# Probabilities times values in products of 512 queries: high parts in one run, low parts in another, and a head's written order anew on three engines

## The chip, the core and the metric

The kernel runs on one core of a Trainium2 chip. It is one launch of a two-layer encoder, and the metric is the device time of that launch in microseconds (us). Three runs of the kernel before gave 2706.74, 2706.79 and 2706.95 us, median 2706.79.

The engines named in the rows are PE (TensorE matmul), PEld (its weight loads), DVE (VectorE), ACT (ScalarE), POOL (GpSimd) and SP (which issues the DMAs). Each works through its own list of instructions in the order in which the kernel wrote them, and waits at semaphores for the others.

## The reference

Each of two layers does a mix (attention beside a short convolution), a squared-ReLU MLP and a gated embedding, each between two RMS norms. The change touches only the last lines of the attention:

```
def one_block(args):                       # 128 queries, all 1024 keys, 8 heads
    qn_b, qr_b = args
    sc = (einsum('bqhd,bkhd->bhqk', qn_b, k_nope) + einsum('bqhr,bkr->bhqk', qr_b, k_rope))
    w = softmax(sc * scale, axis=-1)
    return einsum('bhqk,bkhd->bqhd', w, v)
...
attn = latent_attention(q_nope, q_rope, k_nope, k_rope, v)
mix = concatenate([group_rms_norm(attn, ...), group_rms_norm(conv, ...)]) 
x = x + rms_norm(mix @ w_out[i], g_post_mix[i])
```

There are 1024 tokens, 8 heads of 64 value channels, 2 layers. All is float32.

## The kernel before, in words

**Splitting.** Every float32 operand of a matmul is kept as a high part, rounded by ACT (`copy`, line 1665), and a low part, the rest, which DVE computes from the two (line 2156, and line 2402 for the probabilities). A product of two such operands is three matmuls (lines 1146 to 1148).

**A head.** The 1024 queries of a head are 8 steps of 128. For step s, written `x.s` below:
- `score.s` (PE): 6 matmuls of 512 keys into two PSUM banks; banks 0 and 1 for even steps, 2 and 3 for odd ones.
- `least.s` (DVE, line 2395): the minimum of the negated scores over 1024 keys. Then `exp.s` (ACT, line 1877) writes the probabilities `pr` and their sum.
- `turn.s.0`, `turn.s.1` (PE, line 1355): four 128 by 128 transposes each, into bank 4 and bank 5.
- `high.s.b` (ACT, `pth`) and `low.s.b` (DVE, `ptl`, line 2402): the high and the low part of the transposed probabilities, 512 elements a partition each.
- `pv` (PE, lines 1379 and 1380): probabilities times values. The stationary operand is a 128 by 128 piece of `vv`, the moving one `pth` or `ptl`. `vv` holds zeros, the values' high part and their low part side by side, so that one matmul gives high times high in one half of the partitions and low times high in the other.

Before, `pv` takes 256 queries (G, two steps) at a time: 8 chunks of keys, each one matmul with `pth` and one with `ptl`, 128x256. `pv.h.G.part` is half of that, 8 matmuls. `pth` and `ptl` have room for two G, so steps 4 and 5 may be written while the product of steps 2 and 3 is still to come.

After `pv`, for each half t of the queries: `out` (ACT) and `sum` (DVE, line 2416) add the two halves of the partitions, `square` and `sq_high` (ACT) and `sq_low` (DVE) prepare the group norm, `var` (PE, lines 1185 and 1186) sums it, `ln` and `r` (ACT, lines 1924 and 1928) give the factor, `scale` (DVE, line 2427) applies it, and `y` (ACT, then DVE) splits the result. `den` (DVE) turns the sums of the probabilities, which SP sends out and back.

**The order.** Three tables, ATT_PE, ATT_ACT and ATT_DVE (from line 222), say in which order each engine does a head's steps. The first number is the head, relative to the current one: `pv.-1.3.0` belongs to the head before, `score.1.0` to the next. Beside the head's own work they hold the next head's keys and values (`kv`, `k`, `v`, `v_turned`) and queries (`q`, `q_low`), the split of a later head's weights (`unit.0`), and for the last head only the first output products (`mix`) and the split of their weights (`last.7.1` to `last.7.3`; `last.6.0` is in the head before it). Steps of a head that doesn't exist are left out: the first head has no `-1` work, the last no `1` work (`head_steps`, line 353).

**Waits that matter.** `turn.s` waits for `exp.s` and for `low.(s-1)` of its bank. `score.s` waits for `exp.(s-2)`. `mix.0.0` waits for `exp.6` of the last head. `var` waits for `sq_low`. `y` of t = 0 waits until SP's store of the former `y` has landed.

Of the kernel before, what the change touches and what calls it, by code (L numbers as in the profile page):

```python
# [29 lines left out]
HEADS, NOPE, ROPE, V_DIM = 8, 64, 32, 64  # L30
# [186 lines left out]
def steps(text):  # L217

    return [(word.split(".")[0],) + tuple(int(n) for n in word.split(".")[1:]) for word in text.split()]


ATT_PE = steps("""
turn.0.0.0 turn.0.0.1 score.0.2 kv.1.0 score.0.3 turn.0.1.0 turn.0.1.1 pv.-1.3.0 kv.1.1 pv.-1.3.1 turn.0.2.0
turn.0.2.1 score.0.4 pv.0.0.0 turn.0.3.0 turn.0.3.1 score.0.5 pv.0.0.1 var.-1.1 v.1 turn.0.4.0 score.0.6 q.1.0
turn.0.4.1 score.0.7 pv.0.1.0 pv.0.1.1 turn.0.5.0 turn.0.5.1 mix.0.0 q.1.1 turn.0.6.0 turn.0.6.1 mix.0.1
score.1.0 pv.0.2.0 turn.0.7.0 turn.0.7.1 mix.1.0 var.0.0 pv.0.2.1 score.1.1
""")

ATT_ACT = steps("""
high.0.0.0 high.0.0.1 exp.0.1 y.-1.0 v.1.0 k.1.0 last.7.1 exp.0.2 high.0.1.0 high.0.1.1 exp.0.3 v.1.1 k.1.1  # L230
out.-1.1 high.0.2.0 high.0.2.1 square.-1.1 sq_high.-1.1 unit.0 last.6.0 high.0.3.0 high.0.3.1 exp.0.4 ln.-1.1
last.7.2 exp.0.5 v_turned.1 high.0.4.0 high.0.4.1 r.-1.1 q.1.0 exp.0.6 y.-1.1 high.0.5.0 high.0.5.1 exp.0.7
out.0.0 high.0.6.0 high.0.6.1 square.0.0 last.7.3 sq_high.0.0 q.1.1 high.0.7.0 high.0.7.1 exp.1.0 ln.0.0 r.0.0
""")

ATT_DVE = steps("""
scale.-1.0 low.0.0.0 low.0.0.1 least.0.2 k.1.0 last.7.1 least.0.3 low.0.1.0 low.0.1.1 y.-1.0 k.1.1 sum.-1.1
low.0.2.0 low.0.2.1 sq_low.-1.1 least.0.4 low.0.3.0 low.0.3.1 den.0.0 least.0.5 unit.0 last.6.0 last.7.2
v_turned.1 least.0.6 q.1.0 low.0.4.0 low.0.4.1 scale.-1.1 least.0.7 q_low.1.0 low.0.5.0 low.0.5.1 q.1.1
sum.0.0 low.0.6.0 low.0.6.1 den.0.1 last.7.3 sq_low.0.0 least.1.0 q_low.1.1 low.0.7.0 low.0.7.1 y.-1.1  # L240
least.1.1
""")


# [108 lines left out]
def head_steps(h, order):  # L353

    for kind, ahead, *more in order:
        if kind == "last":
            if h == ahead:
                yield (kind, h, *more)
        elif kind == "mix":
            if h == HEADS - 1:  # L360
                yield (kind, h, ahead, *more)
        elif 0 <= h + ahead < HEADS:
            if not (kind in ("score", "exp", "least") and h + ahead == h + 1 == HEADS):
                yield (kind, h + ahead, *more)
# [108 lines left out]
def encoder(nc, x_in, w_units, w_head, p_in, gains, table, consts, out):  # L473
# [5 lines left out]
    def sb(name, shape, dt, where=ctx):  # L479
        return where.enter_context(nc.sbuf_tensor(name, shape, dt))  # L480

    def sem(name):
        return ctx.enter_context(nc.semaphore(name))
# [7 lines left out]
    with ctx:  # L491

        den = sb("den", [P, 2, STEPS], f32)
# [39 lines left out]
        with ExitStack() as att:  # L533
# [19 lines left out]
            vv = sb("vv", [P, 2, 8, 3 * V_DIM], f32r, att)  # L553
            pth = sb("pth", [P, 2, 8, 256], f32r, att)
            ptl = sb("ptl", [P, 2, 8, 256], f32r, att)
# [23 lines left out]
        ps = ctx.enter_context(nc.psum_tensor("ps", [P, 8, HALF], f32))  # L579
# [96 lines left out]
        t_out = sem("t_out")  # L676
        t_hi = sem("t_hi")
        t_lo = sem("t_lo")
        pv_out = sem("pv_out")
        o_sq = sem("o_sq")  # L680
        o_copy = sem("o_copy")
# [230 lines left out]
        def step(L, h, s):  # L912

            return (L * HEADS + h) * STEPS + s
# [228 lines left out]
        def _(pe):  # L1143
# [82 lines left out]
            for L in range(DEPTH):  # L1226
# [37 lines left out]
                for n in range(0 if L else SLOTS, len(IN_OUTS) + 1):  # L1264
                    if n < len(IN_OUTS):
                        w, t = IN_OUTS[n]
# [89 lines left out]
                                                   pr[:, s % 2, (4 * b + c) * P:(4 * b + c + 1) * P], ident)  # L1356
                    last.then_inc(t_out, 1)

                def values(h, a, G, part):

                    H = L * HEADS + h
                    if part == 0:
                        pe.wait_ge(t_lo, 2 * step(L, h, 2 * G + 2))
                    if (h, G, part) == (0, 0, 0):
                        pe.wait_ge(v_zero, L + 1)
                    if (G, part) == (0, 0):
                        if h + 1 < HEADS:
                            pe.wait_ge(k_lo, H * 2 + 4)
                            pe.wait_ge(v_f, H * 2 + 4)
                        else:  # L1370
                            pe.wait_ge(o_ln, H * 2 - 1)
                    if (G, part) == (2, 0):
                        if h + 1 < HEADS:
                            pe.wait_ge(q_f, H * 2 + 4)
                        else:
                            pe.wait_ge(o_ln, H * 2)
                    dst = ps[:, 6 + G // 2, (G % 2) * 256:(G % 2 + 1) * 256]
                    for c in range(4 * part, 4 * part + 4):
                        nc.tensor.matmul(dst, vv[:, a, c, V_DIM:3 * V_DIM], pth[:, G % 2, c, :], start=c == 0, stop=False)  # L1379
                        last = nc.tensor.matmul(dst, vv[:, a, c, 0:2 * V_DIM], ptl[:, G % 2, c, :], start=False, stop=c == 7)  # L1380
                    if part == 1:
                        last.then_inc(pv_out, 1)

                def variances(h, a, t):

                    O = (L * HEADS + h) * 2 + t
                    pe.wait_ge(o_sq_lo, O + 1)
                    two_passes(ps[:, 6 + t, :], ones_r[:, 2 + a, :], *square_parts(h)).then_inc(o_var, 1)
# [20 lines left out]
                def attend(h):  # L1409

                    for kind, o, *n in head_steps(h, ATT_PE):
                        a, H = o % 2, L * HEADS + h
                        if kind == "turn":
                            transposes(o, *n)
                        elif kind == "score":
                            scores(o, a, *n)
                        elif kind == "kv":
                            if n[0] == 0:
                                if h:
                                    pe.wait_ge(o_ln, H * 2 - 1)  # L1420
                                else:
                                    pe.wait_ge(q_f, H * 2 + 2)
                            else:
                                pe.wait_ge(k_lo, H * 2 + 3)
                                pe.wait_ge(v_f, H * 2 + 3)
                            keys_and_values(o, a, n[0], 6)
                        elif kind == "v":
                            pe.wait_ge(t_lo, 2 * step(L, h, 3) + 2)
                            values_by_token(o, a, 0, 5)
                        elif kind == "q":  # L1430
                            if n[0]:
                                pe.wait_ge(q_f, H * 2 + 3)
                            elif h:
                                pe.wait_ge(o_ln, H * 2)
                            queries(o, a, n[0], 7)
                        elif kind == "pv":
                            values(o, a, *n)
                        elif kind == "mix":
                            mix_first(*n)
                        elif kind == "var" and (o, n[0]) != (HEADS - 1, 1):  # L1440
                            variances(o, a, n[0])
# [216 lines left out]
        def _(act):  # L1658
# [115 lines left out]
            for L in range(DEPTH):  # L1774
# [4 lines left out]
                for n in range(8 if L else 0, len(IN_OUTS)):  # L1779
                    w, t = IN_OUTS[n]  # L1780
                    kind, j = kind_of(w)
# [99 lines left out]
                def high_of_transposed(h, s, b):  # L1881
                    G = s // 2
                    act.wait_ge(t_out, 2 * step(L, h, s) + b + 1)
                    if (h, s, b) == (0, 0, 0):
                        act.wait_ge(tap, L * 12 + 12)
                    if (h, s, b) == (0, 2, 0):
                        act.wait_ge(mix_stored, L * MIX_STORED + 128)
                    if s % 2 == 0 and b == 0 and (G >= 2 or h):
                        act.wait_ge(pv_out, (L * HEADS + h) * 4 + G - 1)
                    copy(pth[:, G % 2, 4 * b:4 * b + 4, (s % 2) * P:(s % 2 + 1) * P],  # L1890
                         ps[:, 4 + b, :].rearrange("p (c q) -> p c q", c=4)).then_inc(t_hi, 1)

# [258 lines left out]
        def _(dve):  # L2151
# [98 lines left out]
            for L in range(DEPTH):  # L2250
# [39 lines left out]
                for n in range(8 if L else 0, len(IN_OUTS)):  # L2290
                    w, t = IN_OUTS[n]
                    kind, j = kind_of(w)
# [105 lines left out]
                def low_of_transposed(h, s, b):  # L2398
                    G = s // 2
                    dve.wait_ge(t_hi, 2 * step(L, h, s) + b + 1)  # L2400
                    at = (slice(None), G % 2, slice(4 * b, 4 * b + 4), slice((s % 2) * P, (s % 2 + 1) * P))
                    V.tensor_tensor(ptl[at], ps[:, 4 + b, :].rearrange("p (c q) -> p c q", c=4),  # L2402
                                    pth[at].bitcast(f32), ALU.subtract).then_inc(t_lo, 1)
# [403 lines left out]
```

## Time and profile before

| | |
|---|---|
| median of 3 runs | 2706.79 us |
| the profiled execution | 2706.97 us, its span 2704.9 us |
| PE busy | 2691.4 us, 99% of the span |
| PEld, DVE, ACT busy | 2244.1, 1935.7, 1403.2 us |
| lines 1379 and 1380 (`pv`), PE | 512 matmuls each, 128.1 and 127.2 us busy |
| one 128x256 matmul of `pv`, one 128x512 elsewhere | 285 ns and 390 ns |
| TensorE clock granted | 9 of 10 or more in all 40 slices |

Matmuls are pipelined: the next one starts before the last one's modelled end. What a matmul costs is therefore the distance from its start to the next start, and a short wait of PE may hide between a start and a modelled end. The two attention stretches run from 220.7 to about 495 us and from 1560 to about 1833 us of the span.

### The profile page before, as it was taken

To read this page: it belongs to the slowest core of one execution; us is meant where nothing else is said; L and a number is where in the kernel's file an instruction comes from. 1 tells how busy PE (TensorE), PEld (TensorE's weight loads), DVE (VectorE), ACT (ScalarE), POOL (GpSimd) and SP (SyncE) were. 2 spreads that over 40 slices of the span, in tenths; PEclk is the share of its full clock that TensorE was granted. 3 is DMA by queue.
4 is the path that set the end of the run, shared out by engine and by line. 5 is a ranking of instruction groups with operands and counts; after the bars stand their busy time and mean duration, and the time that the engine had idled before them with its cause. 6 is when DMAs were issued, how large, how long until landed. Compare 5 with 4: busy or idle time off the path is not lost.

```text
span 2704.9 us, 34531 instructions
## 1 busy us (share of the span) xinstructions
PE 2691.4 (99%) x12854; PEld 2244.1 (83%) x12854; DVE 1935.7 (72%) x2677; ACT 1403.2 (52%) x2412; POOL 302.7 (11%) x329
## 2 busy tenths in 40 slices
PE   9999999999999999999999999999999999999999
PEld 7888888888888888888888888888888888888886
DVE  5468888476676666688866788893856676667886
ACT  5338888564333333356644488884633333333464
POOL 0230000001111101120003200000011111112000
PEclk9999999999999999999999999999999999999999
DMA  4211112532111111133232111133311111111422
GB/s 167 78 68 41 34 35 74 184 110 71 63 47 55 39 53 57 63 117 117 86 118 75 60 41 34 29 140 124 140 47 48 63 47 55 39 53 57 148 94 78
DMA packets 85941, 206.17 MB, mean 76 GB/s; under 512 B 8976, under 2 KB 37776, under 8 KB 84752
## 3 DMA queue, kind: packets, MB, share of 16 engines
q1 hardware_dynamic: 85776, 203.97, 22.3%
q8 instruction: 103, 1.69, 0.3%
q14 instruction: 62, 0.51, 0.1%
HBM read 172.42 MB, written 31.52 MB: 75 GB/s over the span
## 4 chain that ended last, share of the span: by engine, by line
PE 94%; DVE 4%; ACT 1%; issue 0%; DMA 0%; POOL 0%; SPq 0%; ACTq 0%; DVEq 0%; POOLq 0%
PE ps L1146 28%; PE ps L1148 28%; PE ps L1147 28%; PE ps L1355 4%; PE ps L1380 2%; PE ps L1379 2%; DVE wl L2156 1%; DVE nm L2395 1%; PE ps L1185 1%; PE ps L1186 1%; DVE ptl L2402 1%; PE ps L1320 0%; ACT hh L1665 0%; DVE xf L2210 0%; PE ps L1172 0%
## 5 line engine op out<-in xcount | busy, mean ns | idle before, releaser
L1146 PE MATMUL ps<-hh,wh 128*128 128x512 f32 x2160 | 845.1, 391 | 2.3 <-DVE hl L2192 1.9
L1148 PE MATMUL ps<-hh,wl 128*128 128x512 f32 x2160 | 841.4, 390 | 0.0
L1147 PE MATMUL ps<-hl,wh 128*128 128x512 f32 x2160 | 841.3, 389 | 0.0
L1665 ACT ACTIVATE wh<-raw 128x256 fp32r<-128x256 f32 (+2 forms) x510 | 318.7, 632 | 481.3 <-PE ps L1148 276.8
L2156 DVE TENSOR_TENSOR wl<-raw,wh 128x256 fp32r<-128x256 f32 (+2 forms) x510 | 366.0, 733 | 160.7 <-ACT wh L1665 160.3
L1146 PEld LDWEIGHTS ps<-hh,wh 128*128 128x128 f32 x2160 | 405.8, 188 | 87.9 <-DVE wl L2156 2.9
L1147 PEld LDWEIGHTS ps<-hl,wh 128*128 128x128 f32 x2160 | 405.8, 188 | 84.6 <-issue 1.4
L1148 PEld LDWEIGHTS ps<-hh,wl 128*128 128x128 f32 x2160 | 405.7, 188 | 84.2
L2580 DVE TENSOR_TENSOR xf<-xf,ps 128x1024 f32<-128x1024 f32 x196 | 238.5, 1218 | 122.9 <-PE ps L1148 122.7
L1146 PE MATMUL ps<-hx,wh 128*128 128x512 f32 x448 | 174.7, 390 | 0.1
L1147 PE MATMUL ps<-hx,wh 128*128 128x512 f32 x448 | 174.4, 389 | 0.0
L1148 PE MATMUL ps<-hx,wl 128*128 128x512 f32 x448 | 174.4, 389 | 0.0
L2402 DVE TENSOR_TENSOR ptl<-ps,pth 128x512 fp32r<-128x512 f32 x256 | 163.8, 680 | 8.6 <-ACT pth L1665 7.9
L1665 ACT ACTIVATE pth<-ps 128x512 fp32r<-128x512 f32 x256 | 140.2, 594 | 48.0 <-PE ps L1355 46.1
L2395 DVE TENSOR_REDUCE nm<-ps 128x1 f32<-128x1024 f32 x128 | 155.4, 1214 | 1.5 <-PE ps L1148 1.1
L1877 ACT ACTIVATE pr<-ps,nm 128x1024 f32<-128x1024 f32 x128 | 142.7, 1115 | 14.5 <-DVE nm L2395 12.6
L1355 PE MATMUL ps<-cst,pr 128*128 128x128 f32 x1024 | 137.6, 274 | 1.1 <-DVE ptl L2402 0.9
L1379 PE MATMUL ps<-pth,vv 128*128 128x256 f32 x512 | 128.1, 285 | 0.0
L1355 PEld LDWEIGHTS ps<-cst,pr 128*128 128x128 f32 x1024 | 116.5, 140 | 14.0 <-issue 2.9
L1380 PE MATMUL ps<-ptl,vv 128*128 128x256 f32 x512 | 127.2, 283 | 0.0
L2699 POOL TENSOR_TENSOR spare<-raw 128x256 f32<-128x256 f32 x56 | 44.0, 785 | 722.7 <-DMA raw<-w_units 722.7
L1702 ACT ACTIVATE sq<-xf 128x512 f32<-128x512 f32 x168 | 102.8, 622 | 39.4 <-DVE accy L2186 12.3
(240 smaller groups left out, 4304.4 us busy)
## 6 DMA issues: line engine op xcount, KB each, us to landing
raw<-w_units SPq DMA_DIRECT2D x170, 512.0 KB, 3.4
raw<-w_units SPq DMA_DIRECT2D x112, 256.0 KB, 3.0
x_mid<-xf SPq DMA_DIRECT2D x4, 2048.0 KB, 7.9
xf<-x_mid SPq DMA_DIRECT2D x4, 2048.0 KB, 8.1
hh<-mix_hi SPq DMA_DIRECT2D x14, 512.0 KB, 6.1
hl<-mix_lo SPq DMA_DIRECT2D x14, 512.0 KB, 6.8
stage<-w_head SPq DMA_DIRECT2D x16, 320.0 KB, 3.3
mix_hi<-cyh SPq DMA_DIRECT2D x8, 512.0 KB, 2.6
```

The source lines that it names most:

```text
L1146: nc.tensor.matmul(dst, ah, bh, start=start, stop=False, skip_group_check=joins)
L1147: nc.tensor.matmul(dst, ah, bl, start=False, stop=False, skip_group_check=joins)
L1148: return nc.tensor.matmul(dst, al, bh, start=False, stop=stop, skip_group_check=joins)
L1355: last = nc.tensor.transpose(ps[:, 4 + b, c * P:(c + 1) * P], pr[:, s % 2, (4 * b + c) * P:(4 * b + c + 1) * P], ident)
L1379: nc.tensor.matmul(dst, vv[:, a, c, V_DIM:3 * V_DIM], pth[:, G % 2, c, :], start=c == 0, stop=False)
L1380: last = nc.tensor.matmul(dst, vv[:, a, c, 0:2 * V_DIM], ptl[:, G % 2, c, :], start=False, stop=c == 7)
L1665: return nc.scalar.activation(dst, src, ACT.Copy, **more)
L1877: nc.scalar.activation(pr[:, s % 2, :], ps[:, 2 * (s % 2):2 * (s % 2) + 2, :].rearrange("p b n -> p (b n)"), ACT.Exp, bias=nm[:, s % 2:s % ...
L2156: return V.tensor_tensor(dst, whole, high.bitcast(f32), ALU.subtract)
L2395: V.tensor_reduce(nm[:, s % 2:s % 2 + 1], ps[:, 2 * (s % 2):2 * (s % 2) + 2, :].rearrange("p b n -> p (b n)"), AX.X, ALU.min).then_inc(s_l ...
L2402: V.tensor_tensor(ptl[at], ps[:, 4 + b, :].rearrange("p (c q) -> p c q", c=4), pth[at].bitcast(f32), ALU.subtract).then_inc(t_lo, 1)
L2580: V.tensor_tensor(f, f, ps[:, bank:bank + 2, :], ALU.add).then_inc(down_add, 1)
```

## The change

`pv` becomes two steps, `pv_high.h.t.part` and `pv_low.h.t.part`, each for 512 queries (t) and half of the chunks: four matmuls of 128x512. `pv_high` needs only the high parts, `pv_low` the low ones. Since one product now reads both places of `pth` or `ptl`, the two places are no longer used in turns: ACT may write the next steps' high parts after `pv_high` of the same chunks, DVE the low parts after `pv_low` (each by halves of the chunks). The three tables are written anew.

```
 ATT_PE = steps("""
-turn.0.0.0 turn.0.0.1 score.0.2 kv.1.0 score.0.3 turn.0.1.0 turn.0.1.1 pv.-1.3.0 kv.1.1 pv.-1.3.1 turn.0.2.0
...
+turn.0.0.0 turn.0.0.1 pv_low.-1.1.0 pv_low.-1.1.1 score.0.2 turn.0.1.0 turn.0.1.1 kv.1.0 score.0.3 turn.0.2.0
...
-                def values(h, a, G, part):
+                def values(h, a, t, part, high):
 
                     H = L * HEADS + h
-                    if part == 0:
-                        pe.wait_ge(t_lo, 2 * step(L, h, 2 * G + 2))
-                    if (h, G, part) == (0, 0, 0):
+                    pe.wait_ge(t_hi if high else t_lo, 2 * step(L, h, 4 * t + 3) + part + 1)
+                    if (h, t, part) == (0, 0, 0):
                         pe.wait_ge(v_zero, L + 1)
-                    if (G, part) == (0, 0):
+                    if (t, part, high) == (0, 0, True):
                         if h + 1 < HEADS:
                             pe.wait_ge(k_lo, H * 2 + 4)
                             pe.wait_ge(v_f, H * 2 + 4)
...
-                    dst = ps[:, 6 + G // 2, (G % 2) * 256:(G % 2 + 1) * 256]
+                    dst = ps[:, 6 + t, :].rearrange("p (g n) -> p g n", g=2)
                     for c in range(4 * part, 4 * part + 4):
-                        nc.tensor.matmul(dst, vv[:, a, c, V_DIM:3 * V_DIM], pth[:, G % 2, c, :], start=c == 0, stop=False)
-                        last = nc.tensor.matmul(dst, vv[:, a, c, 0:2 * V_DIM], ptl[:, G % 2, c, :], start=False, stop=c == 7)
-                    if part == 1:
-                        last.then_inc(pv_out, 1)
+                        if high:
+                            last = nc.tensor.matmul(dst, vv[:, a, c, V_DIM:3 * V_DIM], pth[:, :, c, :], start=c == 0, stop=False)
+                        else:
+                            last = nc.tensor.matmul(dst, vv[:, a, c, 0:2 * V_DIM], ptl[:, :, c, :], start=False, stop=c == 7)
+                    last.then_inc(pv_high if high else pv_out, 1)
...
-                    if s % 2 == 0 and b == 0 and (G >= 2 or h):
-                        act.wait_ge(pv_out, (L * HEADS + h) * 4 + G - 1)
+                    if s % 4 == 0 and (s or h):
+                        act.wait_ge(pv_high, (L * HEADS + h) * 4 + s // 2 - 1 + b)
...
                     dve.wait_ge(t_hi, 2 * step(L, h, s) + b + 1)
+                    if s % 4 == 0 and (s or h):
+                        dve.wait_ge(pv_out, (L * HEADS + h) * 4 + s // 2 - 1 + b)
```

DVE, last head of layer 0, from `last.7.2` on, as it was (`nm` is `least`, `ptl` is `low`, `wl<-raw,wh` is `last`, `of<-of,gv,sq` is `scale`, `of<-of,ps` is `sum`, `hl<-of,hh` is `y`):

```order
L2156 TENSOR_TENSOR wl<-raw,wh 128x1024
L2395 TENSOR_REDUCE nm<-ps 128x1
L2402 TENSOR_TENSOR ptl<-ps,pth 128x4x128 x2
L2427 SCALAR_TENSOR_TENSOR of<-of,gv,sq 64x512
L2395 TENSOR_REDUCE nm<-ps 128x1
L2402 TENSOR_TENSOR ptl<-ps,pth 128x4x128 x2
L2416 TENSOR_TENSOR of<-of,ps 64x512
L2402 TENSOR_TENSOR ptl<-ps,pth 128x4x128 x2
```

The two `nm` rows are `least.6` and `least.7`. `last.7.2` stands ahead of both, and `y` of the head before comes after all of these rows.

The same engine and place as it is now, from `least.6` to `sq_low.0.0` (`wl<-sq,wh` or `yl<-sq,yh`, by the head):

```order
L2395 TENSOR_REDUCE nm<-ps 128x1
L2404 TENSOR_TENSOR ptl<-ps,pth 128x4x128 x2
L2156 TENSOR_TENSOR wl<-raw,wh 128x1024
L2429 SCALAR_TENSOR_TENSOR of<-of,gv,sq 64x512
L2156 TENSOR_TENSOR hl<-of,hh 64x512
L2395 TENSOR_REDUCE nm<-ps 128x1
L2418 TENSOR_TENSOR of<-of,ps 64x512
L2404 TENSOR_TENSOR ptl<-ps,pth 128x4x128 x2
L2156 TENSOR_TENSOR wl<-raw,wh 128x1024
L2412 STREAM_TRANSPOSE dent<-den 128x32
L2414 TENSOR_SCALAR dent<-dent 128x32
L2156 TENSOR_TENSOR yl<-sq,yh 128x512
```

`last.7.2`, `scale` and `y` of the head before now stand between `least.6` and `least.7`, and `last.7.3` between `low.6.1` and `sq_low.0.0`.

PE, first head of layer 0, between `score.0.2` (rows `kl,hh` and `kh,hl`) and `kv.1.0` (rows `hh`, `hl,hh`):

```order
 L1147 MATMUL ps<-kl,hh 128x512
 L1148 MATMUL ps<-kh,hl 128x512
+L1355 MATMUL ps<-cst,pr 128x128 x8
 L1146 MATMUL ps<-hh 128x512
 L1147 MATMUL ps<-hl,hh 128x512
```

`turn.0.1` now follows `score.0.2` at once; before, `kv.1.0` and `score.0.3` stood between them.

## Rows read from the trace of the kernel before

**Rows 1.** The page: the busy time of each engine, and the chain that ended last.

```profile
PE 2691.4 (99%) x12854; PEld 2244.1 (83%) x12854; DVE 1935.7 (72%) x2677; ACT 1403.2 (52%) x2412; POOL 302.7 (11%) x329
...
PE 94%; DVE 4%; ACT 1%; issue 0%; DMA 0%; POOL 0%; SPq 0%; ACTq 0%; DVEq 0%; POOLq 0%
```

**Rows 2.** Window of the first attention stretch: start:end, length, busy PE, PEld, DVE, ACT, POOL.

```profile
220.70:495.00 274.30, 272.64 (x1723) 239.32 (x1722) 239.08 (x347) 227.58 (x407) 5.60 (x16) 1.00 0.20 64
```

**Rows 3.** Timeline of PE, 306 to 313 us: start, duration, engine, line.

```profile
306.36 0.39 PE L1146 MATMUL ps<-hh 128*128 128x512 f32 x1
...
308.17 0.39 PE L1148 MATMUL ps<-hh,hl 128*128 128x512 f32 x1
...
310.23 0.28 PE L1379 MATMUL ps<-pth,vv 128*128 128x256 f32 x1
...
312.15 1.04 PE L1355 MATMUL ps<-cst,pr 128*128 128x128 f32 x8
312.95 0.48 PE L1146 MATMUL ps<-hh 128*128 128x512 f32 x1
313.26 0.39 PE L1147 MATMUL ps<-hl,hh 128*128 128x512 f32 x1
```

**Rows 4.** Timeline of PE in the last head of layer 0, places where it waits.

```profile
462.14 0.39 PE L1148 MATMUL ps<-kh,hl 128*128 128x512 f32 x1
463.06 0.50 PE L1146 MATMUL ps<-kh,hh 128*128 128x512 f32 x1 [0.54 <-ACT pr L1877]
...
467.23 0.28 PE L1380 MATMUL ps<-ptl,vv 128*128 128x256 f32 x1
467.88 1.22 PE L1355 MATMUL ps<-cst,pr 128*128 128x128 f32 x8 [0.38 <-DVE ptl L2402]
...
476.93 0.60 PE L1355 MATMUL ps<-cst,pr 128*128 128x128 f32 x4
477.86 0.50 PE L1146 MATMUL ps<-kh,hh 128*128 128x512 f32 x1 [0.33 <-ACT pr L1877]
```

**Rows 5.** Timeline of DVE in the last head of layer 0.

```profile
468.26 0.67 DVE L2156 TENSOR_TENSOR hl<-of,hh 64x512 fp32r<-64x512 f32 x1
...
476.74 1.23 DVE L2156 TENSOR_TENSOR wl<-raw,wh 128x1024 fp32r<-128x1024 f32 x1 [0.33 <-ACT wh L1665]
477.89 1.22 DVE L2395 TENSOR_REDUCE nm<-ps 128x1 f32<-128x1024 f32 x1
479.02 1.28 DVE L2402 TENSOR_TENSOR ptl<-ps,pth 128x512 fp32r<-128x512 f32 x2
480.22 0.73 DVE L2427 SCALAR_TENSOR_TENSOR of<-of,gv,sq 64x512 f32<-64x512 f32 x1
```

**Rows 6.** Timeline of ACT in the last head of layer 0.

```profile
475.67 1.05 ACT L1665 ACTIVATE wh<-raw 128x1024 fp32r<-128x1024 f32 x1
...
477.70 1.06 ACT L1665 ACTIVATE pth<-ps 128x512 fp32r<-128x512 f32 x2
...
479.18 1.11 ACT L1877 ACTIVATE pr<-ps,nm 128x1024 f32<-128x1024 f32 x1
```

**Rows 7.** Timeline of three engines in the first head of layer 0.

```profile
220.69 1.03 PE L1355 MATMUL ps<-cst,pr 128*128 128x128 f32 x8
...
222.29 1.12 ACT L1877 ACTIVATE pr<-ps,nm 128x1024 f32<-128x1024 f32 x1
...
223.23 1.28 DVE L2402 TENSOR_TENSOR ptl<-ps,pth 128x512 fp32r<-128x512 f32 x2
...
228.24 1.23 PE L1355 MATMUL ps<-cst,pr 128*128 128x128 f32 x8 [0.15 <-DVE ptl L2402]
```

**Rows 8.** Timeline around 357 us, a middle head: PE, SP's queue and ACT.

```profile
356.80 1.03 PE L1355 MATMUL ps<-cst,pr 128*128 128x128 f32 x8
...
358.00 0.60 SPq L1068 DMA_DIRECT2D mix_lo<-yl  x1
...
360.76 0.63 ACT L1665 ACTIVATE yh<-of 64x512 fp32r<-64x512 f32 x1 [0.99 <-DMA mix_lo<-yl]
```

More of the change, by code:

```diff
@@ L222 @@
 ATT_PE = steps("""
-turn.0.0.0 turn.0.0.1 score.0.2 kv.1.0 score.0.3 turn.0.1.0 turn.0.1.1 pv.-1.3.0 kv.1.1 pv.-1.3.1 turn.0.2.0
-turn.0.2.1 score.0.4 pv.0.0.0 turn.0.3.0 turn.0.3.1 score.0.5 pv.0.0.1 var.-1.1 v.1 turn.0.4.0 score.0.6 q.1.0
-turn.0.4.1 score.0.7 pv.0.1.0 pv.0.1.1 turn.0.5.0 turn.0.5.1 mix.0.0 q.1.1 turn.0.6.0 turn.0.6.1 mix.0.1
-score.1.0 pv.0.2.0 turn.0.7.0 turn.0.7.1 mix.1.0 var.0.0 pv.0.2.1 score.1.1
+turn.0.0.0 turn.0.0.1 pv_low.-1.1.0 pv_low.-1.1.1 score.0.2 turn.0.1.0 turn.0.1.1 kv.1.0 score.0.3 turn.0.2.0
@@ L227 @@
+turn.0.2.1 score.0.4 kv.1.1 turn.0.3.0 turn.0.3.1 score.0.5 pv_high.0.0.0 pv_high.0.0.1 v.1 turn.0.4.0 pv_low.0.0.0
+pv_low.0.0.1 var.-1.1 turn.0.4.1 score.0.6 turn.0.5.0 turn.0.5.1 q.1.0 score.0.7 mix.0.0 turn.0.6.0 turn.0.6.1
+q.1.1 mix.0.1 score.1.0 turn.0.7.0 turn.0.7.1 mix.1.0 score.1.1 var.0.0 pv_high.0.1.0 pv_high.0.1.1
 """)
 ATT_ACT = steps("""
-high.0.0.0 high.0.0.1 exp.0.1 y.-1.0 v.1.0 k.1.0 last.7.1 exp.0.2 high.0.1.0 high.0.1.1 exp.0.3 v.1.1 k.1.1
-out.-1.1 high.0.2.0 high.0.2.1 square.-1.1 sq_high.-1.1 unit.0 last.6.0 high.0.3.0 high.0.3.1 exp.0.4 ln.-1.1
@@ L232 @@
-last.7.2 exp.0.5 v_turned.1 high.0.4.0 high.0.4.1 r.-1.1 q.1.0 exp.0.6 y.-1.1 high.0.5.0 high.0.5.1 exp.0.7
-out.0.0 high.0.6.0 high.0.6.1 square.0.0 last.7.3 sq_high.0.0 q.1.1 high.0.7.0 high.0.7.1 exp.1.0 ln.0.0 r.0.0
+high.0.0.0 high.0.0.1 exp.0.1 y.-1.0 high.0.1.0 high.0.1.1 exp.0.2 v.1.0 k.1.0 last.7.1 high.0.2.0 high.0.2.1 exp.0.3
+out.-1.1 v.1.1 k.1.1 high.0.3.0 high.0.3.1 exp.0.4 unit.0 last.6.0 square.-1.1 sq_high.-1.1 v_turned.1 high.0.4.0
+exp.0.5 high.0.4.1 ln.-1.1 r.-1.1 last.7.2 high.0.5.0 high.0.5.1 exp.0.6 y.-1.1 q.1.0 out.0.0 high.0.6.0 high.0.6.1
@@ L234 @@
+exp.0.7 square.0.0 last.7.3 sq_high.0.0 q.1.1 high.0.7.0 high.0.7.1 exp.1.0 ln.0.0 r.0.0
 """)
 ATT_DVE = steps("""
[L237 to L240, printed above, removed]
@@ L241 @@
-least.1.1
+scale.-1.0 low.0.0.0 low.0.0.1 y.-1.0 least.0.2 low.0.1.0 low.0.1.1 least.0.3 k.1.0 last.7.1 low.0.2.0 low.0.2.1
+least.0.4 sum.-1.1 k.1.1 low.0.3.0 low.0.3.1 least.0.5 unit.0 last.6.0 sq_low.-1.1 v_turned.1 low.0.4.0 den.0.0
+low.0.4.1 least.0.6 low.0.5.0 low.0.5.1 last.7.2 scale.-1.1 q.1.0 y.-1.1 least.0.7 q_low.1.0 sum.0.0 low.0.6.0
+low.0.6.1 q.1.1 last.7.3 den.0.1 sq_low.0.0 least.1.0 low.0.7.0 low.0.7.1 least.1.1 q_low.1.1
 """)
@@ L678, in encoder @@
         t_lo = sem("t_lo")
+        pv_high = sem("pv_high")
         pv_out = sem("pv_out")
@@ L1371, in values @@
                             pe.wait_ge(o_ln, H * 2 - 1)
-                    if (G, part) == (2, 0):
+                    if (t, part, high) == (1, 0, True):
                         if h + 1 < HEADS:
@@ L1435, in attend @@
                             queries(o, a, n[0], 7)
-                        elif kind == "pv":
-                            values(o, a, *n)
+                        elif kind in ("pv_high", "pv_low"):
+                            values(o, a, *n, kind == "pv_high")
                         elif kind == "mix":
```

## The prediction, made before the changed kernel ran

> **What bounds the kernel.** I read the page first: PE is busy for 99% of the span, and the chain that ended last runs through PE for 94% of it [rows 1]. So only PE's own list counts: what its instructions cost, and where it has to wait. The window of an attention stretch comes second. PE is busy for 272.6 of 274.3 us there, DVE for 239.1 (87%) and ACT for 227.6 (83%) [rows 2]. DVE and ACT keep up, with little to spare, and they work in order: one early step that is not ready holds back all behind it. Third, the timeline of PE, start to start. Nine matmuls of 512 columns in a row start 0.226 us apart (1.81 over 8), the 16 of 256 columns in `pv` 0.120 us apart (1.92 over 16), eight transposes take 0.80, and the first matmul after transposes costs 0.31 instead of 0.23 [rows 3].
>
> **The products.** 1024 matmuls of 256 columns go, 512 of 512 columns come. A pair cost 2 x 0.120 = 0.240, its successor 0.226: 0.014 x 512 = 7.2 us less. Matmuls that follow transposes run at about 0.23, and half of `pv_low` now stands there. Were all at 0.232, the gain would be 4.1. I take 6.2. The moving operand is now two pieces of 256, which no row shows; if that costs as two matmuls, the gain is 0. The columns streamed are the same, so more than 7.2 can't come. Groups of transposes stay nine a head, so the switches cost the same.
>
> The same rows bear on a rule of the Trainium skill ("TensorE: Matmul & The Clock Gate", section "Wait — 56ns, not 53.3ns?"): at full clock a matmul costs its columns at 2.4 GHz and a fixed 2.5 ns or so. By it the change is worth 512 x 2.5 ns = 1.3 us. The trace differs: 0.226 and 0.120 are both some 13 ns above their columns. The sum goes by the rows.
>
> **Middle heads.** I lay the new order out with the trace's durations, from `turn.0` at zero, all in us after it. PE needs 34.0 a head, where the stretch of before is 274.3 / 8 = 34.3 [rows 2]. What each step waits for comes earlier, in most places by 0.7 or more. The new waits for the single buffer are covered: `low.0.0` and `low.0.1` on DVE now wait for `pv_low` (1.8 and 2.7 after `turn.0`), with `y` and `least.2` queued behind, but `score.2` ends only at 4.1; `turn.1`, which waits for `low.0.1` (to 3.6), comes at 4.1; ACT's `high.4` follows `turn.4`, which stands behind `pv_high` on PE anyway. The narrow ones: `kv.1.1` at 10.0 (`k.1.0` on DVE now follows `least.3` and ends at 9.8), `pv_high.0.0` at 13.6 (`k.1.1` at 13.4), `turn.5.1` at 21.2 (`low.4.1` at 20.9), and `turn.2`, which comes 7.7 after `turn.0`. ACT's `y.-1.0` waits there for SP's store of the former `y`: it started 3.96 after `turn.0` and 2.76 after the store's issue, having idled 0.99 [rows 8]. The store stays where it is in SP's list, behind a read that waits for `ln`, at the same place against `turn.0`. But `high.1`, `exp.2` and, through DVE's `y`, `least.2` stand behind it. From a start Y: ACT 0.63, DVE 0.67, `least.2` 1.22, `exp.2` 1.12 [rows 5, 6] and 0.3 of latencies end at Y + 3.9, so `turn.2` waits once Y is past 3.8. Ten heads have this wait; at 0.1 to 0.2 each it is 1.5. Of the 1.7 that PE isn't busy in the stretch [rows 2], 1.4 is shown in [rows 4, 7]; the other 0.3 a layer lies in middle heads and goes with the old order, and about half as much again that a modelled end hides: 0.9 in all. Net +0.6.
>
> **First head of each layer.** `turn.0` starts at 220.69, `score.0.2` takes until 222.95, and there `turn.1` now wants to start, 2.7 earlier than `kv` and `score.3` would let it. It needs `exp.1` (222.29 + 1.12 = 223.41) and both `low.0` (the second ends at 223.23 + 1.28 = 224.51) [rows 7], neither moved by the change. So `turn.1.1` starts at 224.65 instead of 223.35: 1.3 lost. The wait of before, at 228.24 (0.15 shown, 0.3 start to start, and 0.2 to 0.3 more inside, its eight transposes being 1.23 long instead of 1.03 [rows 7]), goes. Net +0.7 a layer, +1.4 in all.
>
> **Last head of each layer.** It has no `kv`, no `q` and no next scores to stand between a score and its `turn`, and it has three weight splits (1.05 on ACT, 1.23 on DVE [rows 5, 6]). What hid the chains elsewhere is gone.
> - `score.2` ends at 4.1 and `turn.2` is wanted at 6.4. `least.2` (from 4.3) and `exp.2` end at 6.8: 0.6 lost. With `last.7.1` on ACT ahead of `high.2`, `exp.3` ends at 9.85 for a `turn.3` wanted at 9.25: 0.75 lost.
> - Then from `turn.4.1`, zero again. PE would reach `mix.0.0` at 4.1, `turn.6` at 5.5, `turn.7` at 8.4 (score 1.47, transposes 0.80, `mix` 1.37 and 2.13). ACT: `high.4.1` to 1.2, `ln`, `r` to 2.4, `last.7.2` to 3.4, two `high.5` to 4.4, `exp.6` to 5.4, for which `mix.0.0` waits. DVE: `low.5` (1.28) to 5.15, `last.7.2` (1.23) to 6.3, `scale` (0.73) to 7.0; ACT's `y` (0.63) to 7.65; DVE's `y` (0.67) to 8.4; `least.7` (1.22) to 9.6; `exp.7` (1.12) to 10.8; `sum` and two `low.6` until 11.4. `turn.7` so ends at 11.95 instead of 9.2: 2.75 lost. Before, `least.7` stood ahead of `y`, and `last.7.2` ahead of `least.6`.
> - Behind `exp.7`: `square` (0.63), `last.7.3` on ACT (1.05) and DVE (1.23), `den` 0.4, `sq_low` 0.69: 14.7, where `var.0.0` is wanted at 13.4: 1.4 lost.
>
> Together 5.5. The same head waited 1.9 before: 462.14 to 463.06 is 0.7 above the usual distance, 467.23 to 467.88 0.5 and its transposes 0.2, 476.93 to 477.86 0.5 [rows 4]. Net +3.6 a layer, +7.2 in all. What follows (products of `mix`) has 5.5 us of PE work between the last `pv_low` and `var`, against 3.5 of chain, so nothing is given back or added there. The bounds: +11 if nothing of it is hidden, -4 if nothing waits, the old waits included.
>
> **Sum.** From the profiled execution, 2706.97 (span 2704.9 and 2.1 around it): -6.2 + 0.6 + 1.4 + 7.2 = +3.0, 2710.0. The median of the runs is 0.2 below that execution, so 2709.8; I say 2710.
>
> **Rivals.**
> - *The waits of the last head don't come.* For: its chain crosses engines three times, and a few steps earlier on DVE would close the gap; before, the same head lost but 1.9 with `last` steps in it. Against: DVE's order is fixed, with `scale` and `y` ahead of `least.7`. With as little waiting as before: 2706.8 - 6.2 + 1.4 + 0.6 = 2702.6; with none at all, in the middle either, 2699. 14%.
> - *The middle heads take to waiting (slower).* `y.-1.0` waits for the store, and now `least.2` waits for `y`. Decides from Y = 3.8 on. The one case in view is 3.96; at 4.8, 0.9 is lost in each of ten heads. With 0.5 to 0.9 in ten heads the time is 2714 to 2718, say 2716. For: DVE at 87%; against: the other places have slack, and SP's read isn't later than before. 22%.
> - *The longer matmul saves nothing*, because the two pieces of its moving operand cost as two: +6.2, 2716. For: no row has such an operand; against: the switch from one instruction to the next is all that the 13 ns can be. A saving as small as by the skill's rule above would give nearly the same, 2715. 9%.
> - My forecast has the remaining 55%, with its own range of 2706 to 2713.
>
> **The numbers.** What this kernel's measurement tells from no change is 0.2%, 5.4 us: faster below 2701.4, slower above 2712.2. Faster: most of the first rival's lower part and a little more, 0.11. Slower: the second and third rivals nearly whole (0.28) and the forecast's upper end (0.06), 0.34. Same: 0.55. The range, 2702 to 2717, takes in the first rival's usual case and the means of the two others.
>
> **What would show it.** `pv` in the changed trace: 1024 rows fewer by 512, of 512 columns, starting 0.226 to 0.232 apart; 0.240 is the third rival. PE in the first heads: `turn.1` released by DVE's `low`, about 1 us late. In the last heads: PE idle before `mix.0.0` or `turn.7` released by `exp`, and before `var` by `sq_low`, together some 5 us a layer. If PE waits at `turn.2` in many middle heads it is the second rival, and middle heads should otherwise be 0.3 to 0.5 us shorter than 34.3. I am wrong in the main step if the last head waits for less than 3 us.

## The result, and the profile after

The changed kernel takes 2710.68 us (median of 20 runs, 2709.12 to 2711.57), the kernel before 2707.11 in the same comparison (20 runs). The ratio is 1.0013 with an interval of [1.0007, 1.0019]: 3.6 us slower, within the 0.2% that was called no change, though the interval leaves out 1. The forecast was 2710.0. The profiled execution took 2711.56 us, with a span of 2709.8.

The page of the changed kernel, its first and fourth part and two groups of the fifth. They answer to [rows 1]:

```profile
PE 2687.2 (99%) x12342; PEld 2210.8 (82%) x12342; DVE 1937.5 (72%) x2677; ACT 1405.2 (52%) x2412; POOL 297.4 (11%) x329
...
PE 92%; DVE 3%; ACT 2%; issue 1%; DMA 0%; SPq 0%; POOL 0%; ACTq 0%; DVEq 0%; POOLq 0%
...
L1146 PE MATMUL ps<-hh,wh 128*128 128x512 f32 x2160 | 845.2, 391 | 5.3 <-ACT pr L1877 2.6
...
L1355 PE MATMUL ps<-cst,pr 128*128 128x128 f32 x1024 | 137.5, 274 | 6.6 <-DVE ptl L2404 3.8
```

PE has 512 matmuls fewer (12854 before) and 4.2 us less to do, and the kernel is slower. The share of the chain that runs through PE fell from 94 to 92%, and matmuls that hardly waited before now wait for `exp` (`ACT pr`) and for `low` (`DVE ptl`). PE gained work time and lost it again by waiting.

The last head of layer 0 on PE, where most of it is lost; it answers to [rows 4] (start, duration, and in brackets the idle time shown and its releaser):

```profile
463.45 1.04 PE L1355 MATMUL ps<-cst,pr 128*128 128x128 f32 x8
...
465.48 0.40 PE L1148 MATMUL ps<-kh,hl 128*128 128x512 f32 x1
466.32 1.09 PE L1355 MATMUL ps<-cst,pr 128*128 128x128 f32 x8 [0.45 <-ACT pr L1877]
...
468.42 0.40 PE L1148 MATMUL ps<-kh,hl 128*128 128x512 f32 x1
469.34 1.11 PE L1355 MATMUL ps<-cst,pr 128*128 128x128 f32 x8 [0.53 <-ACT pr L1877]
...
480.12 0.40 PE L1148 MATMUL ps<-kh,hl 128*128 128x512 f32 x1
481.80 0.48 PE L1146 MATMUL ps<-hh,wh 128*128 128x512 f32 x1 [1.28 <-ACT pr L1877]
...
485.97 0.39 PE L1148 MATMUL ps<-hh,wl 128*128 128x512 f32 x1
487.30 1.23 PE L1355 MATMUL ps<-cst,pr 128*128 128x128 f32 x8 [0.94 <-DVE ptl L2404]
...
489.52 0.40 PE L1148 MATMUL ps<-hh,wl 128*128 128x512 f32 x1
490.94 0.50 PE L1185 MATMUL ps<-yh,ones_r 128*128 128x512 f32 x1 [1.02 <-DVE yl L2156]
```

The lateness of a step is the distance from the start before it to its own start, less the usual 0.23: `turn.2` comes 0.61 late, `turn.3` 0.69, `mix.0.0` 1.45, `turn.7` 1.10 and its transposes 0.18 more, `var.0.0` 1.19. That is 5.2 us, and 5.2 again in the last head of layer 1. Before it was 1.9 each.

The first head of layer 0, which answers to [rows 7]; `turn.1` is 1.12 late by the same reckoning, and its transposes take 0.2 longer:

```profile
223.62 0.39 PE L1148 MATMUL ps<-kh,hl 128*128 128x512 f32 x1
224.97 1.22 PE L1355 MATMUL ps<-cst,pr 128*128 128x128 f32 x8 [0.96 <-DVE ptl L2404]
```

The rest of the account, all from starts on PE: the first head of each layer got 0.6 longer (from the first group of line 1320 to the next, 20.36 us before, 20.95 and 20.97 after); a middle head without a late `turn.2` takes 34.06 instead of 34.28. From the first line 1320 of an attention stretch to its last `var`, layer 0 went from 283.8 to 285.0 us and layer 1 from 283.1 to 285.6, 3.8 together. The remaining 1.1 of the 4.9 between the two spans lies outside these two stretches; a second profile of the changed kernel has 2.6 in them and 2.7 between the spans, so it isn't due to the change.

### The profile page after: what moved, and what is told of

It reads as the page before. It is cut to its first block, busy times and chain, and to the rows that moved or that the text cites. A ratio compares the mean times of both kernels' runs of the same rounds, so it can differ in the third digit from the quotient of the medians.

```text
span 2709.8 us, 33569 instructions
## 1 busy us (share of the span) xinstructions
PE 2687.2 (99%) x12342; PEld 2210.8 (82%) x12342; DVE 1937.5 (72%) x2677; ACT 1405.2 (52%) x2412; POOL 297.4 (11%) x329
## 4 chain that ended last, share of the span: by engine, by line
PE 92%; DVE 3%; ACT 2%; issue 1%; DMA 0%; SPq 0%; POOL 0%; ACTq 0%; DVEq 0%; POOLq 0%
PE ps L1146 28%; PE ps L1148 28%; PE ps L1147 27%; PE ps L1355 3%; PE ps L1379 2%; PE ps L1381 2%; DVE nm L2395 1%; PE ps L1185 1%; ACT wh L1665 1%; DVE wl L2156 1%; PE ps L1186 1%; ACT pr L1877 0%; ACT hh L1665 0%; DVE ptl L2404 0%; PE ps L1320 0%
## 5 line engine op out<-in xcount | busy, mean ns | idle before, releaser
L1355 PEld LDWEIGHTS ps<-cst,pr 128*128 128x128 f32 x1024 | 117.9, 140 | 29.8 <-ACT pr L1877 13.4
L1146 PE MATMUL ps<-kh,hh 128*128 128x512 f32 x256 | 106.1, 415 | 0.4 <-issue 0.4
L1148 PE MATMUL ps<-kh,hl 128*128 128x512 f32 x256 | 100.7, 393 | 0.0
```

The costliest lines, as they stand in the source:

```text
L1146: nc.tensor.matmul(dst, ah, bh, start=start, stop=False, skip_group_check=joins)
L1148: return nc.tensor.matmul(dst, al, bh, start=False, stop=stop, skip_group_check=joins)
L1355: last = nc.tensor.transpose(ps[:, 4 + b, c * P:(c + 1) * P], pr[:, s % 2, (4 * b + c) * P:(4 * b + c + 1) * P], ident)
```

## Experiments

Each is compared with the kernel before on its own chip; their medians there were 2706.86, 2706.89 and 2706.93. Sums over both layers are meant where "in all" stands.

### The width of the products undone (e1_two_of_256)

```
+                        for g in range(2):
                             if high:
-                                last = nc.tensor.matmul(dst, ..., pth[:, :, c, :], start=c == 0, stop=False)
+                                last = nc.tensor.matmul(dst[:, g, :], ..., pth[:, g, c, :], start=c == 0 and g == 0, ...)
```

> The changed kernel with its new order and waits, but each product of 512 queries issued as two matmuls of 256 columns with the same stationary piece. The product width is the only thing undone. Theory: a pair of 256 costs 0.240 us start to start and one of 512 costs 0.229 in the changed trace, so 512 x 0.011 = 5.6 us come back, less 0.5 for waits that the slower PE hides: 2707.1 + 3.6 + 5.1 = 2715.8, 8.7 above the kernel before. Rival (the width is worth nothing, or 1.3 us by the fixed cost that the skill states): 3.6 to 4.9 above.

Measured: 2714.45 us, ratio 1.0029 [1.0018, 1.0041], 7.6 above the kernel before, where 8.7 was expected, and 3.9 above the changed kernel (2710.52 when it ran again). First PE of this kernel, then of the changed kernel:

```profile
320.58 2.07 PE L1380 MATMUL ps<-pth,vv 128*128 128x256 f32 x16
322.50 0.71 PE L1355 MATMUL ps<-cst,pr 128*128 128x128 f32 x5
```

```profile
320.90 1.99 PE L1379 MATMUL ps<-pth,vv 128*128 128x512 f32 x8
322.73 1.03 PE L1355 MATMUL ps<-cst,pr 128*128 128x128 f32 x8
```

Sixteen of 256 columns take 1.92 us, eight of 512 take 1.83: 0.011 each, 5.8 us over 512. This pair of groups is at the wide end: summed over all product matmuls of a kernel, from each start to the next start on PE, it is 126.3 us here and 121.7 in the changed kernel, 4.6 apart. The medians say 3.9. The five waits of the last heads are the same in this kernel, to 0.02 us. So they belong to the order, not to the width: the order alone costs 7.6 us, the width gives 3.9 back.

### The last head: the weight splits moved (e2_last_units)

```
+    if order is ATT_DVE and h == HEADS - 1:
+        order = moved(order, ('last', 7, 2), ('low', 0, 7, 1))
+        order = moved(order, ('last', 7, 3), ('last', 7, 2))
+    elif order is ATT_ACT and h == HEADS - 1:
+        order = moved(order, ('last', 7, 2), ('high', 0, 7, 1))
+        order = moved(order, ('last', 7, 3), ('r', 0, 0))
```

> The changed kernel, in the last head only: the weight splits last.7.2 and last.7.3 moved behind high.7.1 and r on ACT and behind low.7.1 on DVE; y stays ahead of least.7. Theory A (the splits make the last head late): its waits fall from 5.2 to about 2.2 us a layer; mix.0.0 waits about 0.65 instead of 1.45, turn.7 about 0.2 instead of 1.3, var not at all; 6 us less in all, 2704.7, 2.4 below the kernel before. Theory B (y ahead of least.7 does it): mix.0.0 0.65, but turn.7 still 1 us late; 3 to 4 us less.

Measured: 2705.49 us, ratio 0.9995 [0.9986, 1.0003], 5.0 below the changed kernel. PE of this kernel at `mix.0.0`, at `turn.7` and at the last `var`:

```profile
479.32 0.40 PE L1161 MATMUL ps<-kh,hl 128*128 128x512 f32 x1
480.26 0.47 PE L1159 MATMUL ps<-hh,wh 128*128 128x512 f32 x1 [0.54 <-ACT pr L1890]
...
484.68 1.22 PE L1368 MATMUL ps<-cst,pr 128*128 128x128 f32 x8
...
496.42 0.39 PE L1161 MATMUL ps<-hh,wl 128*128 128x512 f32 x1
497.10 0.50 PE L1198 MATMUL ps<-yh,ones_r 128*128 128x512 f32 x1 [0.29 <-DVE yl L2169]
```

`mix.0.0` is 0.71 late, `turn.7` starts on time (only its second half waits, 0.18), `var.0.0` doesn't wait. A new wait of 0.45 stands at the last `var`: on DVE and ACT the splits now lie in front of the steps that it needs (`last.7.3` on DVE runs from 490.18 to 491.41, `scale` after it). Theory A has it, with 0.8 less gain than it promised.

### The last head: `y` behind `least.7` (e3_last_y)

```
+    if order is ATT_DVE and h == HEADS - 1:
+        order = moved(order, ('y', -1, 1), ('least', 0, 7))
```

> The changed kernel, in the last head only: DVE's y of the head before moved behind least.7; the weight splits stay. Theory A (the splits): waits fall from 5.2 to about 4.4 us a layer; mix.0.0 still 1.45, turn.7 0.65, var 1.0; 1.6 us less in all, 2709.1. Theory B (y): turn.7 no longer waits and var waits less than 0.5; 4 us less, 2706.7.

Measured: 2709.49 us, ratio 1.0011 [1.0002, 1.002], 1.0 below the changed kernel run again. PE of this kernel:

```profile
480.43 0.48 PE L1155 MATMUL ps<-hh,wh 128*128 128x512 f32 x1 [1.28 <-ACT pr L1886]
...
485.36 1.09 PE L1364 MATMUL ps<-cst,pr 128*128 128x128 f32 x8 [0.37 <-ACT pr L1886]
...
489.29 0.50 PE L1194 MATMUL ps<-yh,ones_r 128*128 128x512 f32 x1 [1.45 <-DVE yl L2165]
```

`mix.0.0` is as late as before, `turn.7` 0.53 late instead of 1.28, and `var.0.0` 1.61 instead of 1.19: half of what `turn.7` gained is lost at the next wait, since `last.7.3` and `sq_low` follow at their own pace. Expected had been 1.0 there. Theory B would have needed 4 us; it falls. By the waits of the last head, the splits are worth 2.6 us a layer and `y` 0.3; by the medians 5.0 and 1.0 in all. The 1.0 is no more than single runs scatter (2708.43 to 2711.50 here), but it is far from 4.

### Both edits of the last head (e4_last_both)

> Both edits of the last head together: splits moved to the end of the head, y behind least.7. Expected waits of the last head: turn.2 0.6, turn.3 0.7, mix.0.0 0.65, turn.7 and var none: 2.0 a layer instead of 5.2, 6.4 us less in all, 2704.3, 2.8 below the kernel before (ratio 0.9990). If the time of the change has another cause than the waits of the last head, the waits vanish from the trace and the time stays at 2710.

Measured: 2705.12 us, ratio 0.9994 [0.9985, 1.0002], 5.4 below the changed kernel. PE at `mix.0.0`, `turn.7` and the last `var`:

```profile
480.34 0.47 PE L1160 MATMUL ps<-hh,wh 128*128 128x512 f32 x1 [0.54 <-ACT pr L1891]
...
484.75 1.04 PE L1369 MATMUL ps<-cst,pr 128*128 128x128 f32 x8
...
496.31 0.39 PE L1162 MATMUL ps<-hh,wl 128*128 128x512 f32 x1
497.17 0.50 PE L1199 MATMUL ps<-yh,ones_r 128*128 128x512 f32 x1 [0.47 <-DVE yl L2170]
```

`turn.7` waits for nothing now. What is left is 0.6, 0.7 and 0.7 as expected, and 0.63 at the last `var`, which wasn't, so the time is 0.8 above the 2704.3 expected. 5.2 less 2.6 a layer is 5.2 in all, and the medians say 5.4: the waits of the last head are the time.

### The swap of `least.2` and `y` (e5_mid_swap), beside the changed kernel again (e6_after_again)

```
-scale.-1.0 low.0.0.0 low.0.0.1 y.-1.0 least.0.2 low.0.1.0 ...
+scale.-1.0 low.0.0.0 low.0.0.1 least.0.2 y.-1.0 low.0.1.0 ...
```

> The changed kernel with two neighbours swapped in DVE's order of every head: least.2 ahead of y.-1.0. Theory (the store of y holds least.2, exp.2 and so turn.2 in some middle heads): the waits of PE at turn.2 in middle heads of the changed trace, 0.14, 0.27, 0.69, 0.33 and 0.13, 1.6 in all, go: 1.6 us less than the changed kernel, 2709.1; last head as it is or 0.1 shorter at turn.2. Rival (those waits have another cause, as ACT's own late start): they stay, no difference.

> The changed kernel itself, to have it on the same chip as its relatives: 3.6 above the kernel before, as first measured; its trace should show the same waits in the last heads (5.2 a layer) and the first (1.1), while those of the middle heads, which hang on when a DMA lands, may differ by some tenths.

Measured: the changed kernel 2710.52, ratio 1.0012 [1.0003, 1.0021]; with the swap 2709.27, ratio 1.0008 [1.0, 1.0017]. The cause, in a middle head of layer 1 of the changed kernel (the first profile), four engines in turn; it answers to [rows 8]:

```profile
1663.56 1.03 PE L1355 MATMUL ps<-cst,pr 128*128 128x128 f32 x8
...
1671.96 1.09 PE L1355 MATMUL ps<-cst,pr 128*128 128x128 f32 x8 [0.53 <-ACT pr L1877]
```

```profile
1664.00 1.69 SPq L1068 DMA_DIRECT2D mix_hi<-yh  x1
1665.74 0.60 SPq L1068 DMA_DIRECT2D mix_lo<-yl  x1
```

```profile
1668.18 0.63 ACT L1665 ACTIVATE yh<-of 64x512 fp32r<-64x512 f32 x1 [1.80 <-DMA mix_lo<-yl]
...
1670.70 1.12 ACT L1877 ACTIVATE pr<-ps,nm 128x1024 f32<-128x1024 f32 x1 [0.93 <-DVE nm L2395]
```

```profile
1668.85 0.68 DVE L2156 TENSOR_TENSOR yl<-of,yh 64x512 fp32r<-64x512 f32 x1 [1.62 <-ACT yh L1665]
1669.46 1.21 DVE L2395 TENSOR_REDUCE nm<-ps 128x1 f32<-128x1024 f32 x1
```

`y` starts 4.62 after `turn.0` and `turn.2` 3.78 after `y`, 0.69 late. In the other nine middle heads of that profile with this wait `y` came 3.8 to 4.3 after `turn.0` and `turn.2` up to 0.33 late, from nothing at 3.75 and 0.02 at 3.83 to 0.27 at 4.08 and 0.33 at 4.26. In the second profile two heads lost 0.28 and one 0.14. With the swap no middle head is more than 0.05 late at `turn.2`. But in the last head, where `low.1` is followed closely by `turn.2` and `turn.3`, the swap puts `y` in front of it, and `turn.3` is 1.02 late with 0.18 inside, instead of 0.70. So the rival falls. By the distances between line 1320 and line 1320, the middle heads gain 2.2 against the first profile of the changed kernel and 1.1 against the second, and the last heads lose 1.0, where the sum hadn't looked; the medians are 1.25 apart.

### All edits (e7_all), and all but the last head's swap (e9_all_but_last_swap)

```
+    elif order is ATT_PE and h == 0:
+        order = moved(order, ('kv', 1, 0), ('score', 0, 2))
```

> Last head's splits and y moved as in the run with both, the swap of least.2 and y in every head, and in the first head of a layer kv.1.0 on PE ahead of turn.1. In the first head turn.1 then waits for nothing (1.1 less), but exp.2 comes 0.6 late for turn.2, so 0.5 a layer is won. Sum: 2705.1 - 1.6 - 1.0 = 2702.5, 4.4 below the kernel before (ratio 0.9984).

> The kernel with all edits, but least.2 stays behind y.-1.0 in the last head, where the swap made turn.3 wait 1.0 us (and its transposes 0.2 longer) instead of 0.7. Theory: 0.5 a layer comes back, 1.0 in all: 2703.55 - 1.0 = 2702.6, 4.3 below the kernel before (ratio 0.9984).

Measured: 2703.55, ratio 0.9987 [0.9978, 0.9996], and 2702.56, ratio 0.9984 [0.9975, 0.9993]. Both intervals leave out 1, though the differences are under the 0.2% that was called no change: the second kernel is 4.4 us faster than the kernel before, and 8.0 faster than the changed kernel. The first missed its 2702.5 by the 1.0 that the swap costs in the last heads; the second, without it, has it. PE of the second in the first head, which answers to [rows 7]:

```profile
225.08 1.04 PE L1372 MATMUL ps<-cst,pr 128*128 128x128 f32 x8
...
227.96 1.09 PE L1372 MATMUL ps<-cst,pr 128*128 128x128 f32 x8 [0.45 <-ACT pr L1894]
```

`turn.1` follows `kv.1.0` without a wait; `turn.2` is 0.61 late for `exp.2`, as expected. Before the edit `turn.1` alone cost 1.3, 0.2 of it inside its transposes. The first head went from 20.95 to 20.29 us in both layers.

### The width again, with the waits out of the way (e10_same_with_256)

> The same kernel with each product of 512 queries issued as two matmuls of 256 columns: the width of the products alone, now with little waiting in the way. By the traces 8 matmuls of 512 take 1.83 us (1.91 behind transposes) and 16 of 256 take 1.92 (1.99): 0.0105 a matmul, 512 x 0.0105 = 5.4 us more than the kernel beside it, less what its waits hide (0.2 to 0.6). Rival (width worth 4 or less, as the first pair of medians says): 3.5 to 4 more.

Measured: 2706.45, ratio 0.9998 [0.9989, 1.0007], 3.9 above the kernel beside it, as in the first pair. The period of two middle heads (line 1320 at 303.51 and 371.50 us, here 302.98 and 371.56) is 67.99 with 512 columns and 68.58 with 256: 0.30 a head, 4.7 in sixteen, of which the last `var` takes back 0.24 a layer (0.39 late instead of 0.63). That leaves 4.2. The rival is nearer: the width is worth 4 to 5 us, not 5.4. From the first matmul of a group of products to what PE does next it takes, with 512 columns and with 256: 1.83 and 1.91 where transposes follow, 1.91 and 1.99 where a score follows, 1.93 and 2.00 before `var`, about 1.96 and 2.03 before line 1320. So a group saves 0.07 or 0.08, not the 0.09 that the theory read from one group; over all product matmuls the starts give 4.9 (121.6 against 126.4). Why the medians show 0.3 less than the 4.2 isn't settled; single runs scatter more than that (2702.0 to 2703.9 for the kernel beside it). In a middle head without a wait this kernel takes 34.29 us, as the kernel before did (34.28), and the one beside it 34.0: away from the first and last heads, and with the swap, the new order costs nothing.

### The moving operand in one piece (e8_one_piece)

```
-            pth = sb("pth", [P, 2, 8, 256], f32r, att)
+            pth = sb("pth", [P, 8, 512], f32r, att)
...
                     if (h, s, b) == (0, 0, 0):
+                        act.wait_ge(cv_lo, L * 8 + 8)
+                        act.wait_ge(mix_stored, L * MIX_STORED + 128)
```

> The changed kernel with the high and low parts of the probabilities laid out so that a product's 512 columns lie in one piece; the first write of each layer must then wait for the last convolution's stores, some 4 us more a layer, so its total isn't compared. Theory (two pieces cost nothing): pv_high still starts every 0.229 us. Rival (the piece boundary costs the 2 to 3 ns above the 0.2265 of other products): 0.2265.

Measured: 2727.58 us in a single execution, with `pv_high`:

```profile
328.80 1.99 PE L1379 MATMUL ps<-pth,vv 128*128 128x512 f32 x8
330.62 1.03 PE L1355 MATMUL ps<-cst,pr 128*128 128x128 f32 x8
```

1.82 for eight against 1.83: two pieces cost nothing that shows. What the early wait did instead is told at the end.

## Why the prediction was right, point by point

- **The sum** was +3.0 and the measured difference 3.6, with the sign and the mechanism as forecast. That the two lie so close is in part luck: the products gave some 1.3 to 2.3 less than forecast, and the last heads (0.6 in all), the first heads (0.2) and the middle heads cost less than forecast, which cancels a part of it.
- **The products** were put at 6.2, with bounds 0 and 7.2. The two pairs of medians give 3.9, the starts of all product matmuls 4.6 and 4.9. The term was over-sized by 1.3 to 2.3: the 7.2 behind it took the fastest row of 512 columns (0.226), while `pv_high` runs at 0.229 and `pv_low` behind transposes at 0.24 a matmul. The 4.1 that the prediction gave for matmuls all at 0.232 was nearer. The rival that two pieces cost as two fell. By the fixed 2.5 ns a matmul that the Trainium skill states ("TensorE: Matmul & The Clock Gate", "Wait — 56ns, not 53.3ns?"), an estimate is 1.3 us; measured is three times that.
- **The last head** was put at 5.5 a layer and is 5.2; net +3.6 against +3.3. The chain holds nearly to the tenth. From the start of `turn.4.1` (476.27) the forecast had `exp.6` done at 5.4, `least.7` at 9.6, `exp.7` at 10.8, `low.6` at 11.4, `var.0.0` at 14.8 (13.4 and 1.4 lost); the rows of the changed kernel say 5.3, 9.4, 10.6, 11.5 and 14.7. DVE there:

```profile
478.29 1.23 DVE L2395 TENSOR_REDUCE nm<-ps 128x1 f32<-128x1024 f32 x1
480.12 1.29 DVE L2404 TENSOR_TENSOR ptl<-ps,pth 128x512 fp32r<-128x512 f32 x2 [0.60 <-ACT pth L1665]
481.32 1.22 DVE L2156 TENSOR_TENSOR wl<-raw,wh 128x1024 fp32r<-128x1024 f32 x1
482.45 0.74 DVE L2429 SCALAR_TENSOR_TENSOR of<-of,gv,sq 64x512 f32<-64x512 f32 x1
483.89 0.68 DVE L2156 TENSOR_TENSOR hl<-of,hh 64x512 fp32r<-64x512 f32 x1 [0.70 <-ACT hh L1665]
484.50 1.21 DVE L2395 TENSOR_REDUCE nm<-ps 128x1 f32<-128x1024 f32 x1
```

  One place was wrong in the telling: I had all of the loss at `turn.7`. `mix.0.0` waits for `exp.6`, so 1.45 fell there and 1.28 at `turn.7`; the sum (2.73 for 2.75) is the same, since `exp.7` doesn't hang on PE.
- **The first head**: +0.7 a layer forecast, +0.6 measured, at `turn.1` and for `low` as said.
- **The middle heads**: net +0.6 forecast. 1.8 of late `turn.2` in one profile, 0.9 in the other, against the 1.5 I had put down; the waits of before that went are 1.3 (what its middle heads took over 34.28) against 0.9. So the net is +0.5 or -0.4, by profile. The bound of 3.8 after `turn.0`, from which `y` makes `turn.2` late, holds. The period fell by 0.22, and by 0.28 with the swap, where 0.39 was due from the products alone. The mechanism of the slower rival is real, but its price is a quarter of what it needed.
- **The rival without the last head's waits** had 2702.6, and the order that takes most of them away, and those of the other heads with them, runs at 2702.56. The agreement is chance: the rival's sum held the 6.2 of the products, and with the last head's edits alone, which are its case, the time is 2705.12.

## What to carry to other kernels

When one engine is busy for 99% of the span, take the price of a changed instruction from start to start, and then lay the new order out for every variant of the loop body, the first and the last iteration above all: what hides a chain in the steady state (the next iteration's work) isn't there at the end. Here merging the products won 4 us and the one order written for all eight heads lost 7.6, most of it (3.3 a layer) in the last head of each layer. Moving three steps of the last head took 5.4 us off; with a step moved in the first head and two swapped in the others as well, 3.6 us slower became 4.4 us faster.

## What the runs showed of the hardware beyond that

The kernel with one-piece operands kept PE waiting for 6.7 us in the first head of each layer. PE of that kernel, and windows of it (start:end, length, busy us of PE, PEld, DVE, ACT, POOL, granted clock, DMA share, GB/s):

```profile
223.27 0.39 PE L1148 MATMUL ps<-kh,hl 128*128 128x512 f32 x1
230.35 1.97 PE L1355 MATMUL ps<-cst,pr 128*128 128x128 f32 x8 [6.70 <-ACT pr L1877]
231.97 0.77 PE L1146 MATMUL ps<-hh 128*128 128x512 f32 x1
...
235.53 0.63 PE L1148 MATMUL ps<-kh,hl 128*128 128x512 f32 x1
235.96 0.44 PE L1146 MATMUL ps<-kh,hh 128*128 128x512 f32 x1
```

```profile
216.00:223.50 7.50, 7.32 (x38) 5.86 (x36) 7.39 (x11) 5.07 (x9) 1.60 (x2) 1.00 0.00 1
223.50:230.30 6.80, 0.15 (x1) 0.00 (x0) 1.92 (x4) 2.18 (x5) 0.00 (x0) 0.67 0.55 202
231.00:236.00 5.00, 5.00 (x17) 4.12 (x16) 2.15 (x4) 3.36 (x6) 0.00 (x0) 0.50 0.00 0
```

After the wait the granted clock is 0.50 (1.2 GHz), and matmuls start 0.43 apart until 235.96. The wait is 5.7 us longer than the one it replaced (6.85 late instead of 1.12), where 4 was expected. From `turn.1` to the next line 1320 PE then takes 14.3 us instead of 11.8 (14.2 in layer 1): the slower clock cost 2.5 and 2.3 on top. That is 16.3 in all, and this execution is 16.0 above the profiled one of the changed kernel. The waits of up to 1.3 us in the changed kernel left the clock at 1.00.

The issue of one and the same store on SP (`mix_hi<-yh`, just after `turn.0`) took 0.58 to 0.60 us in seven of those ten middle heads, 1.69 in the one shown above, and 1.22 and 1.35 in the two where `turn.2` was 0.27 and 0.33 late. In the second profile the two heads that lost 0.28 had 1.22 there, or 1.31 for the low part behind it instead of 0.60. It is such scatter that moved `y`, and with it `turn.2`, from one profile to the next; where it comes from isn't shown.
